# Norms of the delta rule's queries and keys: logarithms taken during the state-space branch, exponentials in one set

## The reference, cut to what matters

```
h = rms_norm_2(x, norm_mix) * (1 + scale_m) + shift_m
m_z, m_xbc, m_dt, sb_qkv, g_qkv, g_a, g_b, g_gate, br_gate = split(h @ w_in)
y_a = mamba2_branch(m_z, m_xbc, m_dt, ...)       # state-space branch; ends in
                                                 # rms norm per group of 256 of (y + xs*d) * silu(z)
y_c = gated_deltanet_branch(g_qkv, g_a, ...)     # delta rule, 4 heads of 128; begins with
                                                 # q, k = l2_norm(q) * 128**-0.5, l2_norm(k)
l2_norm(x)   = x * rsqrt(sum(x*x) + 1e-6)
rms_norm_2   = x * rsqrt(mean(x*x) + 1e-6) * g
```

## Time and profile before

| | us |
|---|---|
| median of 3 runs | 1601.48 (1598.67 to 1601.87) |
| the profiled execution, its own time | 1591.19 |
| its span (first to last instruction) | 1589.3 |
| PE busy | 1483.1 |
| DVE busy | 779.3 |
| ACT busy | 570.2 |
| POOL busy | 294.9 |

### The profile page before, as it was taken

How to read it: one execution, slowest core, us unless ns; L and a number is a source line. 1 busy time by engine, 2 the same in 40 slices (tenths; PEclk the granted TensorE clock), 3 DMA queues, 4 the chain that set the end, 5 groups by cost and what they waited for, 6 DMA issues and landing times.

```text
span 1589.3 us, 28267 instructions
## 1 busy us (share of the span) xinstructions
PE 1483.1 (93%) x11238; PEld 1239.4 (78%) x11238; DVE 779.3 (49%) x1411; ACT 570.2 (36%) x895; POOL 294.9 (19%) x121
## 2 busy tenths in 40 slices
PE   7978999999999999999998989998799999899897
PEld 5857999999858999989997878997566665555554
DVE  4954888548684888544453524552322221221222
ACT  2345555454355555356544114533111111111111
POOL 0021222212201212227861001772000000000000
PEclk9989999999999999998999987998899999999999
DMA  8674555664434555634641211574899999999995
GB/s 305 238 272 153 167 167 168 197 233 153 140 120 143 181 185 185 201 104 139 193 134 54 80 40 41 194 247 183 350 420 427 425 428 428 428 428 427 428 427 226
DMA packets 64609, 375.82 MB, mean 236 GB/s; under 512 B 7296, under 2 KB 7552, under 8 KB 49152
## 3 DMA queue, kind: packets, MB, share of 16 engines
q1 hardware_dynamic: 64512, 374.43, 62.7%
HBM read 373.35 MB, written 1.05 MB: 236 GB/s over the span
## 4 chain that ended last, share of the span: by engine, by line
PE 62%; issue 13%; DMA 11%; DVE 8%; SPq 2%; ACT 2%; POOL 1%; POOLq 0%; DVEq 0%; ACTq 0%
PE lin L673 8%; PE lin L674 8%; PE lin L675 8%; DMA modrow<-in_experts 7%; PE mixp L1304 4%; PE mixp L1308 4%; PE stat L1329 4%; DVE mixers L1945 3%; DMA moe_low<-in_experts 2%; PE lin L692 2%; DMA moe_high<-in_experts 2%; PE stat L1272 1%; PE stat L673 1%; PE mixp L673 1%; PE stat L675 1%
## 5 line engine op out<-in xcount | busy, mean ns | idle before, releaser
L673 PE MATMUL lin<-r_hi,w_hi 128*128 128x256 f32 x1464 | 427.1, 292 | 12.1 <-POOL w_lo L1749 5.1
L674 PE MATMUL lin<-r_lo,w_hi 128*128 128x256 f32 x1464 | 417.1, 285 | 0.0
L675 PE MATMUL lin<-r_hi,w_lo 128*128 128x256 f32 x1464 | 416.9, 285 | 0.0
L673 PEld LDWEIGHTS lin<-r_hi,w_hi 128*128 128x128 f32 x1464 | 283.8, 194 | 19.7 <-POOL w_lo L1749 6.7
L674 PEld LDWEIGHTS lin<-r_lo,w_hi 128*128 128x128 f32 x1464 | 283.9, 194 | 0.9
L675 PEld LDWEIGHTS lin<-r_hi,w_lo 128*128 128x128 f32 x1464 | 283.8, 194 | 0.0
L1753 POOL TENSOR_TENSOR w_lo<-ring,w_hi 128x1024 fp32r<-128x1024 f32 x71 | 175.7, 2488 | 223.0 <-ACT w_hi L1370 222.7
L1782 DVE TENSOR_TENSOR w_lo<-ring,w_hi 128x1024 fp32r<-128x1024 f32 x126 | 155.4, 1238 | 85.8 <-ACT w_hi L1376 66.2
L1749 POOL TENSOR_TENSOR w_lo<-ring,w_hi 128x1024 fp32r<-128x1024 f32 x42 | 108.3, 2578 | 481.0 <-ACT w_hi L1376 298.2
L1376 ACT ACTIVATE w_hi<-ring 128x1024 fp32r<-128x1024 f32 x124 | 129.6, 1048 | 57.4 <-PE mixp L675 49.5
L1370 ACT ACTIVATE w_hi<-ring 128x1024 fp32r<-128x1024 f32 x119 | 124.1, 1050 | 33.8 <-PE lin L675 16.7
(11 more groups left out here) (460 smaller groups left out, 2813.9 us busy)
## 6 DMA issues: line engine op xcount, KB each, us to landing
ring<-in_panels SPq DMA_DIRECT2D x272, 512.0 KB, 3.6
moe_high<-in_experts SPq DMA_DIRECT2D x32, 2048.0 KB, 29.6
moe_low<-in_experts SPq DMA_DIRECT2D x32, 2048.0 KB, 30.3
aring<-in_ada SPq DMA_DIRECT2D x24, 1024.0 KB, 6.3
ring<-in_experts SPq DMA_DIRECT2D x10, 2048.0 KB, 28.0
cst<-in_experts SPq DMA_DIRECT2D x10, 1280.0 KB, 28.6
sq<-in_experts SPq DMA_DIRECT2D x10, 1024.0 KB, 29.2
rs<-in_experts SPq DMA_DIRECT2D x10, 512.0 KB, 30.3
```

What stands on the lines that cost most here:

```text
L673: pe.matmul(o, w_hi[:, slot, c], r[0], start=start, stop=False, skip_group_check=True)
L674: pe.matmul(o, w_hi[:, slot, c], r[1], start=False, stop=False, skip_group_check=True)
L675: return pe.matmul(o, w_lo[:, slot, c], r[0], start=False, stop=stop, skip_group_check=True)
```

## The change

ACT squares q and k together, right after SB4, into the two halves of `sq`; PE makes both sets of sums after SB6, q's into `mixp` and k's into `stat`, ahead of the scores; ACT takes both logarithms after SB6, q's into `rs` and k's into `rs_gk`, which lies in tiles of `ybr` not yet in use. The state-space output is squared and summed as before, its logarithm goes into `rs_ym`, in other tiles of `ybr`. Then one set of three exponentials follows, in the order k, q, state-space output, and DVE multiplies in that order. On PE the panels are regrouped: 2 ahead of the new sums, 2 behind them, 3 ahead of the sums of the state-space output, and GG0 to GG3 behind those.

```diff
+        rs_ym, rs_gk = ybr[:, 4:6, :], ybr[:, 8:12, :]
...  TensorE
-            linear(None, 4)
+            linear(None, 2)
             pe.wait_ge(ev("m_rows_read"), 2)
             pe.wait_ge(ev("m_rows_exp"), 2)
             pe.wait_ge(ev("m_h_copied"), 1)
+            pe.wait_ge(ln_done, seen.now(ln_done))
+            for at, dst in ((0, mixp), (4, stat)):
+                pe.wait_ge(sq_ready, seen(sq_ready))
+                for i in range(4):
+                    mm = pe.matmul(dst[:, i, :], K["ones"], sq[:, at + i, :], start=True, stop=True, skip_group_check=True)
+                mm.then_inc(sums_ready, 1)
+            linear(None, 2)
+            pe.wait_ge(ln_done, seen(ln_done, 2))
             pe.wait_ge(ev("m_scores_ready"), 1)
...
-            linear(None, 2)
+            linear(None, 3)
             pe.wait_ge(ev("m_ym_ready"), 1)
             sums(sq, 2, 2)
-            linear(None, 2)
-            sums(sq, 4, 1)
-            linear(None, 1)
-            sums(sq, 4, 1)
-            linear(None, 2)
+            linear(None, 4)
             pe.wait_ge(ev("g_k_ready"), 1)
...  ScalarE
-            for j in range(1, 11):
+            def log_sums(dst, src, scale):
+                act.wait_ge(sums_ready, seen(sums_ready))
+                act.activation(dst, src, ACT.Ln, bias=K["eps"], scale=scale).then_inc(ln_done, 1)
+                seen(ln_done)
+            def exp_logs(*logs):
+                act.wait_ge(ln_done, seen.now(ln_done))
+                for t in logs:
+                    act.activation(t, t, ACT.Exp, scale=-0.5).then_inc(rs_ready, 1)
+            for j in range(1, 5):
+                take(sq_kv[:, j, :])
+            act.wait_ge(ev("gq_ready"), 1)
+            for at in (0, 4):
+                act.activation(sq[:, at:at + 4, :], gq[:, at:at + 4, :], ACT.Square).then_inc(sq_ready, 1)
+            for j in range(5, 7):
+                take(sq_kv[:, j, :])
+            log_sums(rs[:, :, :], mixp[:, :, :], 1.0)
+            log_sums(rs_gk, stat[:, :, :], 1.0)
+            for j in range(7, 11):
                 take(sq_kv[:, j, :])
             act.wait_ge(ev("m_ym_ready"), 1)
-            norm(ybr[:, 0:4, :], 4, 2, T)
+            act.activation(sq[:, 0:4, :], ybr[:, 0:4, :], ACT.Square).then_inc(sq_ready, 1)
             take(sq_kv[:, 11, :])
-            take(gg[:, 0, :])
-            act.wait_ge(ev("gq_ready"), 1)
-            act.wait_ge(ev("ya_done"), 1)
-            norm(gq[:, 0:4, :], 4, 4, 1)
-            take(gg[:, 1, :])
-            act.wait_ge(ev("g_q_ready"), 1)
-            norm(gq[:, 4:8, :], 4, 4, 1)
-            take(gg[:, 2, :])
-            take(gg[:, 3, :])
+            log_sums(rs_ym, stat[:, 0:2, :], 1.0 / T)
+            exp_logs(rs_gk, rs[:, :, :], rs_ym)
+            for j in range(4):
+                take(gg[:, j, :])
...  VectorE
+            dve.wait_ge(ev("gq_ready"), 1)
+            dve.wait_ge(rs_ready, seen(rs_ready))
+            dve.tensor_tensor(gq[:, 4:8, :], gq[:, 4:8, :], rs_gk, ALU.mult).then_inc(ev("g_k_ready"), 1)
+            dve.wait_ge(rs_ready, seen(rs_ready))
+            dve.scalar_tensor_tensor(gq[:, 0:4, :], gq[:, 0:4, :], P ** -0.5, rs[:, :, :], ALU.mult, ALU.mult).then_inc(ev("g_q_ready"), 1)
             dve.wait_ge(ev("m_ym_ready"), 1)
             dve.wait_ge(rs_ready, seen(rs_ready))
             for j in range(4):
-                ins = dve.scalar_tensor_tensor(ybr[:, j, :], ybr[:, j, :], col("ssm_norm", j), rs[:, j // 2, :], ALU.mult, ALU.mult)
+                ins = dve.scalar_tensor_tensor(ybr[:, j, :], ybr[:, j, :], col("ssm_norm", j), rs_ym[:, j // 2, :], ALU.mult, ALU.mult)
             ins.then_inc(ev("ya_done"), 1)
-            dve.wait_ge(ev("gq_ready"), 1)
-            dve.wait_ge(rs_ready, seen(rs_ready))
-            dve.scalar_tensor_tensor(gq[:, 0:4, :], gq[:, 0:4, :], P ** -0.5, rs[:, :, :], ALU.mult, ALU.mult).then_inc(ev("g_q_ready"), 1)
-            dve.wait_ge(rs_ready, seen(rs_ready))
-            dve.tensor_tensor(gq[:, 4:8, :], gq[:, 4:8, :], rs[:, :, :], ALU.mult).then_inc(ev("g_k_ready"), 1)
```

More of the change, by code:

```diff
@@ L1659, in _ @@
                 act.activation(r_hi[:, tiles, :], h[:, tiles, :], ACT.Copy).then_inc(r_hi_ready, 1)
[L1661 to L1667, removed]
+            log_sums(rs[:, :, :], mixp[:, :, :], 1.0 / P)
             act.wait_ge(ev("g_o_read"), 1)
             act.activation(sq[:, 0:4, :], ybr[:, 8:12, :], ACT.Square).then_inc(sq_ready, 1)
[L1670 to L1674, removed]
+            log_sums(rs_k, stat[:, :, :], 1.0 / P)
+            log_sums(rs_o, mixp[:, :, :], 1.0 / P)
+            exp_logs(rs[:, :, :], rs_k, rs_o)
             next_split[0] = BRANCHES2
```

## The result

| | before | after |
|---|---|---|
| median of the 5 runs of each, us | 1599.03 (1590.81 to 1601.87) | 1587.32 (1586.91 to 1591.95) |
| profiled execution, us | 1591.19 | 1587.32 |
| its mean granted clock | 0.972 | 0.969 |

The ratio is 0.9944, with a 95% interval of 0.9918 to 0.9969: faster, as forecast, by 5 to 13 us. So the sign and, as will be seen, the local size were right, and the level was not. Three distances have to be kept apart: the medians are 11.7 us apart, the profiled executions 3.9 us, and the forecast was 7.5.

A forecast was written before the change was run, and what follows sets the result against it. The stretch was taken as bound by the order of things, not an engine: TensorE's stalls at the norms. Removing all 7.5 us: 1601.48 - 7.5 = 1594.0 us, range 1591 to 1597.5.

The forecast's parts named there:

- The stalls: TensorE's three waits ahead of the norms' sums and the transposes, 2.57 + 1.58 + 3.30 = 7.45 us, would all go.
- the layout's own figure: Upper bound of the gain, 7.7 us, from laying out the new order up to TensorE's transposes at 852.4.
- The printed idle of 6.97: Idle the profile prints for TensorE's stalls; a lower bound, since the end of a matmul is modelled.
- Every cover: At each new wait TensorE's other work outlasts what it waits for, by 0.4 to 7 us.
- The thin place: TensorE's state-space sums: ready at 839.0, the square ending at 838.6, covered by 0.4 us only.
- ACT's saving off the path: Two table loads instead of six on ACT, 5.1 us less, none on the path except through stalls already counted.
- The gain reaches the end: Later work hangs on TensorE and the experts' transfers start after the branches, so the whole 7.5 us counts.
- The stretches behind unchanged in length: Expected in the profile after: only chunk states to transposes shortens, by 7.5 us; later stretches keep their length.
- A stall that stays: Rival, 0.10: DVE slowed by POOL, TensorE stalls 1.5 to 3.5 us at the state-space sums; gain 4 to 6 us.
- a gain that is hidden: Rival, 0.08: expert-weight transfers run to their own time, so the 7.5 us is waited for at 1100 us; 1601.5.
- The rival by the clock: Rival, 0.04: TensorE's clock drops some 14 us earlier, at the L1154 wait ending near 930; 5.5 us slower, 1607.
- The median of the three runs is 10.3 us above the profiled execution: Level step: the distance is added unchanged to the profiled execution with the change, 1583.7, giving 1594.0 us.

The follow-up runs named there:

- long group: Kernel before, unchanged: the longer of two groups its repeated runs fall into, three of four runs; mean 1599.4 us.
- short group: Kernel before, unchanged: the shorter of two groups its repeated runs fall into, one run in four; mean 1590.5 us.
- two of its variants: Changed kernel with k's and q's exponentials right behind their logarithms (0.9936), and with two panels instead of three ahead of the state-space sums (0.9958).
- the kernel with its stalls filled: Kernel before with two, one and three products of no use (128x512, result overwritten) in its three TensorE stalls: ratio 1.001, median 1595.82 us.
- the regrouped kernel: Kernel before, norms still in a chain, with 3, 1, 1, 2 panels instead of 2, 2, 1, 2: ratio 1.0018.

## Why the prediction was right in its parts and wrong in its level

*The stalls, 7.45 us and bounds 7.0 to 7.7.* Right: 7.72 us, the upper bound, which was the layout's own figure. The printed idle of 6.97 was the lower bound that it was said to be.

*Every cover.* Right. Sums of q and k at 818.26 (forecast 818.0), scores at 827.55 (827.2), state-space sums at 839.33 (839.0), transposes at 852.57 (852.5). The offset is that of the chunk states. The thin place had 0.4 us and kept it; shortening it by a panel cost 2.64 us.

*ACT's saving off the path.* Right: four table loads less were seen on ACT, and two of them put back cost nothing. The Trainium skill ("ScalarE: Activation LUTs", section "Table sets: the hidden batching unit") has one load for ln followed by exp. In the traces of before and changed each Exp behind an Ln has a load of its own, 1.28 us, so the measurement stands against that rule here.

*The gain reaches the end.* Right, within what the clock lets one see: the means are 8.5 us apart (1596.6 and 1588.1) at mean clocks of 0.9677 and 0.9682, and the 0.0005 of clock account for 0.6 by the line above. That leaves 7.8 or 7.9 us, for 7.7 in A. "The stretches behind unchanged in length" did not hold in the trace: B was 1.7 us longer, by the clock.

*The rivals.* A stall that stays and a gain that is hidden did not come. The rival by the clock had the right mechanism and the wrong weight and place: the clock did fall earlier in the changed kernel's traces, at the wait of L1133 and for 1.7 us, not for 13. It does so in two of five traces of the kernel before as well, so that the change need not be the reason.

*The step that failed* is "The median of the three runs is 10.3 us above the profiled execution; I take that distance as it is". That distance was no constant to be carried over. It was the distance between two groups of runs of the kernel before, and the profiled execution stood in the shorter one. The five traces show part of what it is made of: low clock at the stall that the change removes (2.7 to 2.8 us), low clock in B (1.7), low clock in the first 155 us (some 4 either way from the profiled execution), and 2.1 us by which that execution alone was short between L1154 and the first expert.

The first is lost with the stall. By the traces, a long run of before then gains 7.7 + 2.8 = 10.5 us in A. A run without low clock in the stalls gains 7.7 and loses 1.7 if the clock falls in B. The trace of 1593.98 us and the changed one of 1587.32 us, which begin 0.4 us apart, bear it out: they are 6.7 us apart.

The timed runs agree once their clocks are taken in, by the line of 1.26 us for each 0.001. The mean of the long group is 11.3 us above the changed kernel's, at 0.9657 against 0.9682, which is 3.1 us by the line and leaves 8.2. The mean of the short group is only 2.4 us above, at 0.9722, which hides 5.0 us and makes 7.4. So the 7.7 us of A are in both groups, and what differs between them is low clock.

A forecast from the profiled execution alone, 1583.7, would have missed on the other side by 3.6 us. A mean over both groups, 1596.6 less 7.7, gives 1588.9, against 1588.1 measured, though this mean was taken after the result. The range was too narrow for the same reason. It took the spread of three runs that were all in one group.

What stays open: why the changed kernel has no second group, since the low clock in B is there in both of its traces and in two of its variants, and is missing in three of five traces of before; what the second half of the distance between the groups is; and why the kernel with its stalls filled is slower in the experts' stretch.

## What to carry to other kernels

Lay a serial chain out against the work that covers it, start by start: three norms that share one buffer cost 7.7 us here. Reordering the cover alone gained nothing. Two of the norms moved to where their inputs had long been ready gained 5.1 us, and with the cover reordered as well all 7.7. A batched set of exponentials, or fewer table loads, is worth something only on the path. Before a median is carried over from a profiled execution, compare their clocks and take more than three runs; where the runs fall into groups, say which group the profile is from.

## What the runs showed of the hardware

At or right behind a wait of TensorE of 2.2 to 4.9 us the granted clock fell to its low level (1.2 GHz of 2.4) in some runs and not in others, with the same instructions. At the stall of 3.14 us it did in two of five traces of the kernel before. Behind the wait of 2.22 us at L1130 or L1133 it did in the same two of five, in the trace of the regrouped kernel, in one of two with the stalls filled, and in all four traces of kernels with the new norms that kept the wait: eight of twelve. The products behind it then take twice as long (eight records 3.78 us instead of 1.89), 1.7 to 2.8 us per occurrence.

The Trainium skill ("TensorE: Matmul & The Clock Gate", section "Part 1: The HAM clock gate") has the clock follow the engine's recent activity. The filled waits agree: with products in the same wait, in three traces, it did not fall there. They do not prove it, since it also stayed up in four of the twelve waits that were not filled. So such a hole can cost more than its length, by an amount that a single profile does not show.
